# Layer norms of a two-layer decoder step: where the mean is summed, and how the root is taken

## The reference

```python
def layer_norm(x, g, b):
    mu = jnp.mean(xf, axis=-1, keepdims=True)
    var = jnp.mean(jnp.square(xf - mu), axis=-1, keepdims=True)
    y = (xf - mu) * lax.rsqrt(var + LN_EPS) * g + b
...
hp = layer_norm(DN_ALPHA * hp + mp, ln_g[layer, 0], ln_b[layer, 0])
...
hp = layer_norm(DN_ALPHA * hp + peer_ffn(hp, *pw), ln_g[layer, 1], ln_b[layer, 1])
```

## Time and profile before

| | |
|---|---|
| median of three runs | 4103.33 us (4094.71 to 4107.82) |
| the profiled execution | 4102.13 us, its span 4100.5 us |
| mean granted clock of TensorE | 0.972 of full speed |
| PE busy | 3892.5 us, 95% |
| DVE busy | 2723.9 us, 66% |
| ACT busy | 1169.2 us, 29% |
| POOL busy | 597.0 us, 15% |

### The profile page before, as it was taken

How to read it: one execution, slowest core, us unless ns; L and a number is a source line. 1 busy time by engine, 2 the same in 40 slices (tenths; PEclk the granted TensorE clock), 3 DMA queues, 4 the chain that set the end, 5 groups by cost and what they waited for, 6 DMA issues and landing times. The chain is left out here.

```text
span 4100.5 us, 73515 instructions
## 1 busy us (share of the span) xinstructions
PE 3892.5 (95%) x26757; PEld 3653.1 (89%) x26757; DVE 2723.9 (66%) x4932; ACT 1169.2 (29%) x1573; POOL 597.0 (15%) x591
## 2 busy tenths in 40 slices
PE   8878879999999999999998977999999999999998
PEld 8764779999999998999988577999999999899997
DVE  3633367877776337877776946787777624788887
ACT  2211232233333322222213433233333322222222
POOL 0002000000000015444420000000000003544441
PEclk9978899999999999999998998999999999999999
DMA  3146323335455659988962013333554566999984
GB/s 115 47 163 239 116 96 103 119 129 188 146 168 174 195 170 258 267 259 253 265 179 86 18 52 106 103 124 137 175 169 155 172 204 191 265 264 254 269 264 128
DMA packets 297808, 695.32 MB, mean 170 GB/s; under 512 B 44033, under 2 KB 136322, under 8 KB 297282
## 3 DMA queue, kind: packets, MB, share of 16 engines
q1 hardware_dynamic: 255682, 596.88, 45.4%
q0 software_dynamic: 41984, 96.63, 8.8%
HBM read 559.66 MB, written 133.14 MB: 169 GB/s over the span
## 5 line engine op out<-in xcount | busy, mean ns | idle before, releaser
L1699 PE MATMUL ps<-peer_x_then_r_xh,experts_ul 128*128 128x260 f32 x4096 | 1164.9, 284 | 0.0
L1700 PE MATMUL ps<-experts_over_x_xl,experts_uh 128*128 128x260 f32 x4096 | 1154.8, 282 | 0.0
L1701 PE MATMUL ps<-peer_x_then_r_xh,experts_uh 128*128 128x260 f32 x4096 | 1153.6, 282 | 0.0
L1901 DVE TENSOR_TENSOR experts_ul<-experts_u,experts_uh 128x1024 fp32r<-128x1024 f32 x512 | 626.7, 1224 | 575.2 <-ACT experts_uh L1798 572.8
L1798 ACT ACTIVATE experts_uh<-experts_u 128x1024 fp32r<-128x1024 f32 x512 | 540.9, 1057 | 972.1 <-PE ps L1765 612.9
L1699 PEld LDWEIGHTS ps<-peer_x_then_r_xh,experts_ul 128*128 128x128 f32 x4096 | 771.8, 188 | 0.0
L1701 PEld LDWEIGHTS ps<-peer_x_then_r_xh,experts_uh 128*128 128x128 f32 x4096 | 770.0, 188 | 0.0
L1700 PEld LDWEIGHTS ps<-experts_over_x_xl,experts_uh 128*128 128x128 f32 x4096 | 769.8, 188 | 0.0
L1763 PE MATMUL ps<-experts_over_a_ah,experts_ul 128*128 128x448 f32 x2048 | 751.8, 367 | 7.9 <-DVE experts_over_a_al L2097 7.9
L1764 PE MATMUL ps<-experts_over_a_al,experts_uh 128*128 128x448 f32 x2048 | 751.0, 367 | 0.0
L1765 PE MATMUL ps<-experts_over_a_ah,experts_uh 128*128 128x448 f32 x2048 | 750.9, 367 | 0.0
(11 more groups left out here) (365 smaller groups left out, 5031.9 us busy)
## 6 DMA issues: line engine op xcount, KB each, us to landing
experts_u<-peer_u SPq DMA_DIRECT2D x256, 512.0 KB, 3.5
experts_u<-peer_v SPq DMA_DIRECT2D x256, 512.0 KB, 5.2
hidden<-experts_act SPq DMA_DIRECT2D x256, 260.0 KB, 2.1
gates<-experts_over_b_g SPq DMA_DIRECT2D x112, 512.0 KB, 2.9
experts_act<-hidden SPq DMA_DIRECT2D x256, 224.0 KB, 6.4
experts_over_b_g<-gates SPq DMA_DIRECT2D x64, 512.0 KB, 6.8
experts_over_b_g<-gates SPq DMA_DIRECT2D x64, 384.0 KB, 5.4
mla_ct<-cache POOLq DMA_DIRECT2D x64, 320.0 KB, 6.9
```

Of the source, the lines that this page charges most:

```text
L1699: pe.matmul(o, ul[:, b % 4, c], xh[:, c, h, 0:TH], start=(c == 0), stop=False)
L1700: pe.matmul(o, uh[:, b % 4, c], xl[:, c, h, 0:TH], start=False, stop=False)
L1701: mm = pe.matmul(o, uh[:, b % 4, c], xh[:, c, h, 0:TH], start=False, stop=(c == KC - 1))
L1901: v.tensor_tensor(ul[:, b % 4], u[:, b % 2], uh[:, b % 4].bitcast(F32), ALU.subtract).then_inc(split_done, 1)
```

## The change

For the four norms behind a residual the mean is no longer summed within `layer_norm`.

- In `linear` with a residual VectorE keeps a tile `sums`: cleared once, and each collected block is added to it, behind the `low` of the next weight block; the last one directly behind the last collect. TensorE then multiplies `sums` by `mean_d`, one matmul a half, into banks 6 and 7 (`MEAN`).
- In `peer_experts` TensorE, behind its eight transposes, sums the blocks as their residuals are written (`bank_read`, from the fourth on): for each block 260 and 188 columns, and at the end the last 72 columns of all eight blocks, once the late additions are done (`late_ready`).
- `layer_norm` with `mean=MEAN` starts with the subtraction.
- In all five norms the copy of the variance is gone. The root reads the variance from PSUM with 1e-5 as a bias (a new tile `eps`, allocated behind `mean_d`), and the Newton step that multiplied by the copied variance now adds the constant and multiplies in one instruction that reads PSUM.

```diff
 linear, TensorE:
+                if residual:
+                    pe.wait_ge(added, m + 1)
+                    for h in range(2):
+                        pe.matmul(k.ps[:, MEAN + h, 0:TH], k.mean_d[:], sums[:, h * TH:(h + 1) * TH], start=True, stop=True)
...
 linear, VectorE:
+                def add(i, b):
+                    wait(v, psum_free, 2 * i + b + 3)
+                    wait(v, added, 2 * i + b + 1)
+                    v.tensor_tensor(sums[:], sums[:], out[:, bass.ds(2 * i + b, 1), :].rearrange("p o t -> p (o t)"), ALU.add
+                                    ).then_inc(added, 1)
...
                 if residual:
+                    v.memset(sums[:], 0.0).then_inc(added, 1)
                     v.wait_ge(scaled, 1)
                 with v.Fori(0, m // 2 - 1) as i:
                     for b in range(2):
                         collect(i, b)
                         low(i + 1, b)
+                        if residual:
+                            add(i, b)
                 for b in range(2):
                     collect(m // 2 - 1, b)
+                    if residual:
+                        add(m // 2 - 1, b)
...
 layer_norm, TensorE:
-                for h in range(2):
+                for h in range(2) if mean is None else ():
                     for c in range(KC):
                         mm = pe.matmul(k.ps[:, h, 0:TH], k.mean_d[:], r[:, c, part[h]], start=(c == 0), stop=(c == KC - 1))
...
 layer_norm, VectorE:
-                    v.wait_ge(mean_ready, h + 1)
+                    if mean is None:
+                        v.wait_ge(mean_ready, h + 1)
...
-                    v.wait_ge(var_ready, h + 1)
-                    v.tensor_scalar(var[:, part[h]], k.ps[:, 2 + h, 0:TH], LN_EPS, None, ALU.add).then_inc(var_copied, 1)
                     v.wait_ge(rooted, h + 1)
-                    inverse_root(chain, var[:, part[h]], rstd[:, part[h]], newton[:, part[h]])
+                    root, tmp = rstd[:, part[h]], newton[:, part[h]]
+                    chain(v.reciprocal(root, root))
+                    chain(v.scalar_tensor_tensor(tmp, root, -0.5, root, ALU.mult, ALU.mult))
+                    chain(v.scalar_tensor_tensor(tmp, k.ps[:, 2 + h, 0:TH], LN_EPS, tmp, ALU.add, ALU.mult))
+                    chain(v.scalar_tensor_tensor(root, tmp, 1.5, root, ALU.add, ALU.mult))
...
 layer_norm, ScalarE:
-                    act.wait_ge(var_copied, h + 1)
-                    act.activation(rstd[:, part[h]], var[:, part[h]], ACT.Sqrt).then_inc(rooted, 1)
+                    act.wait_ge(var_ready, h + 1)
+                    act.activation(rstd[:, part[h]], k.ps[:, 2 + h, 0:TH], ACT.Sqrt, bias=k.eps[:, 0:1]).then_inc(rooted, 1)
...
 peer_experts, TensorE, behind the transposes:
+                for n, c in enumerate(chunks):
+                    pe.wait_ge(bank_read, max(n + 1, 4))
+                    pe.matmul(k.ps[:, MEAN, 0:TH], k.mean_d[:], r[:, c, 0:TH], start=(n == 0), stop=(n == KC - 1))
+                    pe.matmul(k.ps[:, MEAN + 1, 0:TD - TH], k.mean_d[:], r[:, c, TH:TD], start=(n == 0), stop=(n == KC - 1))
+                for c in range(KC):
+                    if c % 4 == 0:
+                        pe.wait_ge(late_ready, c // 4 + 1)
+                    pe.matmul(k.ps[:, MEAN + 1, TD - TH:TH], k.mean_d[:], r[:, c, TD:T], start=(c == 0), stop=(c == KC - 1))
```

More of the change, by code:

```diff
@@ L75 @@
 LOW = 3
+MEAN = 6
 LOAD = 5
@@ L189, in _ @@
                 v.memset(k.ones[:], 1.0)
+                v.memset(k.eps[:], LN_EPS)
             @block.gpsimd
@@ L222, in linear @@
         scaled = s.sem("scaled")
+        added = s.sem("added")
+        sums = s.sb("sums", [P, T]) if residual else None
         with s.block() as block:
@@ L317, in inverse_root, with layer_norm @@
     chain(v.scalar_tensor_tensor(root, tmp, 1.5, root, ALU.add, ALU.mult))
-def layer_norm(nc, k, name, r, g, b, out, func, ahead=(), store=None):
+def layer_norm(nc, k, name, r, g, b, out, func, ahead=(), store=None, mean=None):
     with Stage(nc, name) as s:
         sq = s.sb("sq", [P, KC, T])
-        var = s.sb("var", [P, T])
         rstd = s.sb("rstd", [P, T])
         newton = s.sb("newton", [P, T])
+        at = 0 if mean is None else mean
         mean_ready = s.sem("mean_ready")
@@ L330, in layer_norm @@
         var_ready = s.sem("var_ready")
-        var_copied = s.sem("var_copied")
         rooted = s.sem("rooted")
@@ L371, in centre @@
                 def centre(h):
-                    v.wait_ge(mean_ready, h + 1)
+                    if mean is None:
+                        v.wait_ge(mean_ready, h + 1)
                     for c in range(0, KC, 2):
                         rh = r[:, c:c + 2, part[h]]
-                        v.tensor_tensor(rh, rh, bc(k.ps[:, h, 0:TH], 1, 2), ALU.subtract).then_inc(centred, 1)
+                        v.tensor_tensor(rh, rh, bc(k.ps[:, at + h, 0:TH], 1, 2), ALU.subtract).then_inc(centred, 1)
                 centre(0)
@@ L419, in __init__ @@
         self.mean_d = sb("mean_d", [P, P])
+        self.eps = sb("eps", [P, 1])
         self.ones = sb("ones", [P, P])
@@ L1368, in peer_layer @@
         layer_norm(nc, k, f"ln{layer}1", r, f"ln_g{layer}1", f"ln_b{layer}1", k.x, ACT.Identity,
-                   slabs(k, (a["w_pw1"][KC], a["w_pw1"][0])) if layer == 0 else (), a["y"] if layer else None)
+                   slabs(k, (a["w_pw1"][KC], a["w_pw1"][0])) if layer == 0 else (), a["y"] if layer else None, mean=MEAN)
 def peer_experts(nc, k, a, layer, xh, r):
@@ L1487, in peer_experts @@
         bank_read = s.sem("bank_read")
+        late_ready = s.sem("late_ready")
         g_landed = [s.sem(f"g_landed{b}") for b in range(2)]
@@ L2147, in _ @@
                     cs = slice(4 * b, 4 * b + 4)
-                    v.scalar_tensor_tensor(r[:, cs, TD:T], k.x[:, cs, TD:T], ALPHA, y_turn[:, b, :, 0:TG], ALU.mult, ALU.add)
+                    v.scalar_tensor_tensor(r[:, cs, TD:T], k.x[:, cs, TD:T], ALPHA, y_turn[:, b, :, 0:TG], ALU.mult, ALU.add
+                                           ).then_inc(late_ready, 1)
 def pointwise_conv(nc, k, a, y):
@@ L2364, in build @@
                 layer_norm(nc, k, f"ln{layer}0", r, f"ln_g{layer}0", f"ln_b{layer}0", k.x, ACT.Identity,
-                           slabs(k, a["peer_wq"][layer]))
+                           slabs(k, a["peer_wq"][layer]), mean=MEAN)
             peer_layer(nc, k, a, layer)
```

## The result

The changed kernel takes 4114.12 us (median, 4106.05 to 4124.68); the kernel before, on the same chip, 4102.64 (4091.44 to 4109.92). The ratio is 1.0033, interval 1.0022 to 1.0045. The prediction was 4089, in the range 4081 to 4097, with 0.07 for slower: wrong in size and in sign.

What follows compares the result with a forecast made beforehand. It took TensorE's expert loops as unchanged and the norms' serial chain as time to save: 2.9 + 2.9 + 2.1 + 1.1 + 3.3 + 2.1 - 0.4 = 14.0 us off the median of 4103.3, given as 4089, range 4081 to 4097.

Steps and rivals of the forecast that it cites:

- Part 1: Mean after a linear stage (ln00, ln10): running sum ends centring 2.9 us earlier in each.
- Part 2: Mean inside the expert stage: centring ends 2.1 us earlier in ln01, 1.1 us earlier in ln11.
- rival (b): Expert mean gains nothing, late records at 0.164 and a longer barrier: 10.8 us gain, 4092.5; chance 0.10.
- Part 3: Root in all five norms: 0.8 us less in each of four, 2.1 us less in cln.
- The clock: TensorE idles between mean and variance matmuls; a clock fall costs 0 to 4.4 us in all, taken as 0.4.
- rival (a): Clock falls in all four gaps, stays low through the variance's first half: 10 us gain, 4093; chance 0.14.
- Rival (c): Slower: eps tile shifts SBUF addresses, expert loops L1699 to L1701 pay; at 3 ns a record 4126; chance 0.08.
- Rival (d): Means of the four residual norms come no earlier, only the root counts: 5.4 us gain, 4098; chance 0.08.

Runs made afterwards that it cites:

- the kernel with the unused tile: The kernel before with an unused tile of one float (32 bytes) at the place of eps, no instruction changed: ratio 1.0059 to the kernel before.
- the wider tile: The changed kernel with the tile eps 16 elements wide instead of 1, so later tiles move by 64 bytes: ratio 0.9985 to the kernel before.

## Why the prediction was wrong

- **Part 1**, running sum: right. Addition, records, barrier and centring came as worked out; `ln10` gained 3.8 with the root (2.9 + 0.8), `ln00` 2.9, because there the root waited 0.90 us for the variance.
- **Part 2**, expert mean: right in mechanism; with the root `ln01` gained 3.2 (2.1 + 0.8 forecast), `ln11` 0.9 (1.1 + 0.8), where the variance came late. The late columns took 1.90 us where I took 1.6; within the bounds of 1.5 and 2.6. The barrier did not grow: 1.12 before and after in `experts0`. But the gain depends on the old mean. In the profile of before it ran mostly at the lower clock (10.14 us, granted clock 0.50 from 2152 to 2156), and `ln01` took 33.19 us, the most of the seven kernels with these norms (30.28 to 33.19; `ln11` 30.39 to 32.19). In the kernel with the unused tile it ran at the full clock:

```profile
2164.61 7.25 PE L357 MATMUL ps<-peer_x_then_r_r,mean_d 128*128 128x260 f32 x32 [3.50 <-PEq L136]
```

There `ln01` took 30.29, the root of before included, hardly more than the 30.03 of the change. So the two reasons that rival (b) gave did not come, late records at 0.164 and a longer barrier; but what it forecast, no gain from the expert part, is what the times show where the old mean found the clock up (3 of the 14 expert norms in those seven kernels).
- **Part 3**, root: right, 0.86 and 2.2 where 0.8 and 2.1 stood. One statement was wrong without cost: the second root doesn't run right behind the first, it waits 3.03 us for the second half of the variance; it is done before the first affine step could start. And the sign of a first affine step about 4.6 us after the first root was a slip: by the prediction's own steps it is 3.2 + 0.7 = 3.9, and `ln00` shows 3.97.
- **The clock** was mis-sized. It fell in all four norms of this execution, as rival (a) said, but only in `ln00` and `ln11` within the gap. In stretches of 1 us the clock stands after POOL's time; `ln00` and `ln11`:

```profile
519.00:520.00 1.00, 0.88 (x4) 0.41 (x3) 0.00 (x0) 0.00 (x0) 0.00 (x0) 1.00 0.00 0
521.00:522.00 1.00, 0.00 (x0) 0.00 (x0) 1.00 (x3) 0.64 (x2) 0.00 (x0) 0.50 0.44 49
...
4083.00:4084.00 1.00, 0.00 (x0) 0.00 (x0) 0.60 (x1) 0.00 (x0) 0.00 (x0) 1.00 0.00 0
4084.00:4085.00 1.00, 0.18 (x1) 0.19 (x2) 1.00 (x3) 0.87 (x2) 0.00 (x0) 0.50 0.03 8
```

In `ln00` the mean records end at 519.87, and at 521 the clock stands at the lower of its levels, 1.2 GHz instead of 2.4; in `ln11` they end at 4082.28, and it is down by the time the variance begins (4084.82). The chain that ended last shows the price in `ln11`, where the earlier trace rows had the table load ahead of the root:

```profile
4084.82 6.74 PE ps L381 x16
...
4091.58 0.49 ACT ln_rstd L413
```

The timeline has the variance of the other two norms shorter (8.97 us against 9.87 and 10.23), for there the clock fell only behind its start:

```profile
2158.59 8.97 PE L381 MATMUL ps<-ln_sq,mean_d 128*128 128x260 f32 x32 [2.53 <-ACT ln_sq L422]
...
2445.28 8.97 PE L381 MATMUL ps<-ln_sq,mean_d 128*128 128x260 f32 x32 [2.42 <-ACT ln_sq L422]
```

The first half of the variance took 6.74 us in `ln11`, the 6.7 of the prediction, and the root waited for it: 1.27 us in `ln11`, 0.90 in `ln00`. In `ln01` and `ln10` the root followed the table load without a wait. So 2.2 in all, between the 0.4 taken and the 4.4 of rival (a). Net of it the norms gained 13.0 where the sum said 14.0. It is no fixed price: with the moving operands moved too, the clock held through the variance in both expert norms (7.28 us), and with the wider tile in `ln01`; these came out at 30.03 and 30.04, as where it fell late. (The fall that the prediction read 2.6 us behind the last matmul of `experts0` came after 2.5, by its 0.96.)

- **The step that failed** is the one at the head of the prediction, that the change leaves the loops of the expert stages alone: the sum has no term for them. The runs show one in its place. Their pitch rose by 1.07 ns a record and the two loops by 13.8 us, more than the norms gained, because the new tile changed the distance between the operands; with the constant in a spare column the same change took 0.9971 of the time before. Rival (c) named the place (L1699 to L1701) and the point from which it decides, 1.1 ns a record, but got 0.08 because of one row, the taps of L2237. That row did not bear on it: its 186 starts lie 430 ns apart (2280.0 to 2359.5), with 512 columns of plain fp32, and a cost that shows at a pitch of 119 need not show there. The text said that no row showed weight loads at shifted starts, and then priced the unknown by the row that was shown. Its sign was the mean duration of a record (above 284 ns), which rose by 3 ns on one line and by 1 on the others, and doesn't tell the 1.07 of the pitch.
- **What no case held:** the 448-column loop. Its records come in levels: 100 us in the middle of it hold 486 or 495 of TensorE's records in kernels whose operands stand alike (at their distance of before), as in layers 0 and 1 of the kernel with all expert tiles moved (stretches; the count stands in brackets behind the busy time):

```profile
1700.00:1800.00 100.00, 100.00 (x486) 90.83 (x485) 79.01 (x104) 21.24 (x20) 42.55 (x41) 1.00 0.81 250
...
3800.00:3900.00 100.00, 100.00 (x495) 92.67 (x494) 81.06 (x106) 21.23 (x20) 40.67 (x40) 1.00 0.96 261
```

By starts these are 206.7 and 202.7 ns a record, 640 or 629 us a loop. It changes mostly where TensorE had to wait for 0.4 to 5 us, but in the version with the wider tile once from one record to the next, and can then stay for hundreds of us. Two loops that differ by 11 us each would account for much of the spread of single runs, 4083 to 4118 us for the kernel before; that is argued from the profiled executions, not shown. With both weights 32 bytes from the moving operands the levels are 206.7, 204.4 and 200.0; the kernel with both weights moved had 502 records in the first of these stretches:

```profile
1700.00:1800.00 100.00, 100.00 (x502) 93.88 (x501) 84.79 (x109) 22.47 (x22) 42.61 (x42) 1.00 0.95 268
```

What picks a level stays open, and whether the 32 bytes cost this loop anything: the two loops together took 1264 to 1281 us with both weights apart, 1256 to 1278 with the operands alike. So does how much of the 24 us of the unused tile is the level's and not the pitch's. The 260-column loops give 13.8 of it and the linear stages some 2.

- **Rival (d)** did not come. In the versions whose operands stand alike in the expert stages the whole change gives 0.9971 to 0.9985, 6 to 12 us, within or below the 9 to 14 us that the norms gained in the profiles.

## What to carry to other kernels

A new tile, however small, moves what is allocated behind it, and not all of it by the same amount where starts are rounded up: compare the distance between the two operands of the hot matmuls before and after. Here a spare column, or a tile of 64 bytes, for the small constant kept it. Where a trace has no row for a cost and that cost is multiplied by 12,288 records, leave it a chance that fits the ignorance, whatever a row of another kind seems to say. And measure a pipelined loop by the distance of starts, not by the mean duration.

## What the runs showed of the hardware

- The pitch of 260-column records is 119.26 ns when weights and moving operand keep their distance, 119.90 to 120.60 when the distance changes by 32 bytes in some or all records, whether the one or the other was moved.
- The 448-column loop runs at 202.7 or 206.7 ns a record, and at 200.0, 204.4 or 206.7 with both weights 32 bytes from the moving operands, with switches in the middle of the loop.
- Sixteen fp32 records of 72 columns take 1.90 us (0.12 each).
- Behind the mean records TensorE sat idle for 2.17 to 2.54 us, and in all four norms of the changed kernel's profile the granted clock fell from 2.4 to 1.2 GHz, in two of them before the variance began and in two behind its start. After gaps of the same length it held in both expert norms of another version.
